# Two transposes of 256 x 1024 fp32, done by DMA in two-byte halves instead of by TensorE

## The chip, the cores and the metric

The kernel runs on one core of a Trainium2 chip. The metric is the device time of one execution in microseconds; three executions of the kernel before took 959.39 to 959.93 us, with a median of 959.49.

## What is computed

The program runs two transformer blocks, one after the other, on one sequence of 256 tokens and 1,024 channels in fp32. Two places matter for this change: the second block takes in a memory of 256 tokens for its cross-attention, and its last step adds a feed-forward to a residual that is the output. Cut to these:

```python
x = x + 0.5 * swiglu(rms_norm(x), ...)           # first block's second feed-forward ("f2u", "f2d")
h = rms_norm(x)                                  # and on to the second block
...
mn = rms_norm_2(mem, norm_mem)                   # mem: 256 tokens x 1024
xkv = mn @ xa_w_kv
...
h = h + (silu(g_conv) * (fn @ ffn_w_up)) @ ffn_w_down   # last feed-forward ("f3u", "f3d")
return h                                         # 256 tokens x 1024, one row a token
```

## The kernel before

Activations are kept transposed in SBUF: `xT` holds the residual as 8 groups of 128 channels (partitions) by 256 tokens, and every product streams such a tile. Weights come as slabs of 8 x 256 or, in the down projections, 11 x 256 columns; SyncE loads slab `s` into `raw[s % 2]`. For accuracy each fp32 product is made of three: ScalarE rounds a slab into a high part `wh` (`split_hi`), VectorE subtracts it for a low part `wl` (`split_lo`), each in two halves (1,536 and 1,280 columns in a down projection), and TensorE forms ah x wh, al x wh and ah x wl. `wh` and `wl` have two slots as well, so the split of slab `s + 2` follows TensorE's use of slab `s`, and TensorE waits for a half of `wl` before it takes that half up. The instructions of each engine are in the order in which the code writes them; there is no scheduler.

A down projection makes its output in four quarters `q` of 256 channels, each from two slabs, `s + 2 q` and `s + 2 q + 1`, of 66 matmuls each. Each engine goes through the quarters in its own `feed_forward`: in quarter 0 ScalarE and VectorE split slab `s + 2`, with which TensorE begins quarter 1. Hooks named `between` are called in each quarter.

**The memory** lies in `memraw` with tokens on partitions. In the down projection `f2d`, between the first and the second quarter, TensorE transposes it (`memory_in`, which calls `transpose_in`, 16 transposes of 128 x 128) into four PSUM banks; ScalarE (`memory_hi`) and VectorE (`memory_lo`) make the high and low parts `mo`, `mlo` from them in quarters 1 and 2. One quarter's matmuls also have a matmul of 32 columns in them (`narrow`) whose result is not used.

**The residual.** In the last down projection `f3d` the output is made with tokens on partitions, so that it can be stored in rows. The residual `xT` is transposed for it by TensorE (`rows_of_x`, 16 transposes) in the second product of `f3u`, just behind the last update of `xT`. ScalarE (`rows_in`) and VectorE (`rows_added`) copy it from PSUM to `xtok`. In `f3u` TensorE's product needs a free accumulator; it is freed by VectorE's line 2104, which waits for the norm's factor, a reciprocal (line 2063).

Of the kernel before, what the change touches and what calls it, by code (L numbers as in the profile page):

```python
# [18 lines left out]
P = 128  # L19
# [50 lines left out]
def shared_signals():  # L70
# [11 lines left out]
    for kind, signals, each, stages in kinds:  # L82
# [7 lines left out]
        "mixer2_dve": [("e7", 1), ("mem_lo", 4), ("kpe", 1), ("la_lo", 1), ("rho2", 1), ("kv_e", 1), ("kv_rd", 1), ("akv", 1),  # L90
# [6 lines left out]
        "mixer2_pe": [("mem_ps", 4), ("kv_ps", 1), ("uk_ps", 3), ("gl_z", 1), ("uq_ps", 3), ("kq_T", 8),  # L97
# [36 lines left out]
def build(nc, A, consts, out):  # L134
# [5 lines left out]
    with ctx:  # L140
# [91 lines left out]
        rin = sb("rin", [P, 2, 4])  # L232
        ah = sb("ah", [P, DC, T], f32r)
# [6 lines left out]
        with ExitStack() as sc:  # L240
# [26 lines left out]
            with ExitStack() as s2:  # L267
                ch = sb("ch", [P, DC, T], f32r, scope=s2)
                cl = sb("cl", [P, DC, T], f32r, scope=s2)

# [44 lines left out]

        L = [ctx.enter_context(nc.psum_tensor(f"acc{i}", [P, 512], f32)) for i in range(2)]
# [35 lines left out]
        xtok = ytok  # L352
        yl = xn[:, :, :].rearrange("p c t -> p (c t)").rearrange("p (g f) -> p g f", g=2)[:, :, 512:1024]\
# [295 lines left out]
        def _(pe):  # L649
# [82 lines left out]
            def rows_of_x():  # L732

                acc_freed(pe, ACC0["xo"] + 2)
                acc_freed(pe, ACC0["xo"] + 3)
                for b in range(TB):
                    for g in range(2):
                        for c in range(4):
                            ins = nc.tensor.transpose(Q[1 + 2 * b + g][:, c * P:(c + 1) * P],
                                                      xT[:, 4 * g + c, b * P:(b + 1) * P], ident)  # L740
                        ins.then_inc(S("res_ps"), 1)

            def late(st):

                if st == "n8":
                    return lambda k: k == 6 and (rows_of_x(), norm_spread(st))
                return lambda k: k == 6 and norm_spread(st)
# [54 lines left out]
            def opening(name, st, xh, xl, extra=None):  # L802
# [51 lines left out]
            def feed_forward(up, down, st, between=None, tokens=False):  # L854
# [13 lines left out]
                for q in range(4):  # L868
# [583 lines left out]
        def _(act):  # L1452
# [279 lines left out]
            def memory_hi(q):  # L1732

                if q == 0:
                    act.wait_ge(*signal("mem_in", 16))
                    for b in range(TB):
                        if b:
                            act.wait_ge(*signal("mem_sq", b))
                        A_(stmp[:, :, :].rearrange("p a t -> p (a t)"), memraw[:, b, :], ACT.Square, scale=1.0 / 32,
                           accum_out=ms7[:, b:b + 1]).then_inc(S("mem_sq"), 1)  # L1740
                elif q < 3:
                    for j in (2 * q - 2, 2 * q - 1):
                        act.wait_ge(*signal("mem_ps", j + 1))
                        for c in range(2):
                            ins = A_(mo[:, 2 * j + c, :], Q[2 + j][:, c * T:(c + 1) * T], ACT.Copy, scale=col(V_MEM + 2 * j + c))
                        ins.then_inc(S("mem_hi"), 1)
# [280 lines left out]
        def _(dve):  # L2027
# [64 lines left out]
            def feed_forward(up, down, st, conv=False, low=None, between=None):  # L2092
# [52 lines left out]
                looped(dve, FP, body, peel=2 if conv else 1)  # L2145
                s, n = SLAB0[down], ACC0[down]
# [21 lines left out]
            def rows_added(q):  # L2168
# [3 lines left out]
                if q == 0:  # L2172
                    for k in range(2):
                        dve.wait_ge(*signal("res_ps", 2 * k + 2))
                        V.tensor_copy(xtok[:, k, 512:D], Q[2 + 2 * k][:, :]).then_inc(S("rows_d"), 1)
                    dve.wait_ge(*signal("rows_a", 2))
                    dve.wait_ge(*signal("rows_d", 2))
# [330 lines left out]
            def memory_lo(q):  # L2508

                if q == 0:  # L2510
                    dve.wait_ge(*signal("mem_sq", 2))
                    V.tensor_scalar(e7[:, :], ms7[:, 0:2], EPS, EPS, ADD, MUL).then_inc(S("e7"), 1)
                elif q < 3:
                    for j in (2 * q - 2, 2 * q - 1):
                        dve.wait_ge(*signal("mem_hi", j + 1))
                        for c in range(2):
                            k = 2 * j + c
                            ins = V.scalar_tensor_tensor(mlo[:, k, :], Q[2 + j][:, c * T:(c + 1) * T], col(V_MEM + k), f(mo[:, k, :]), MUL, SUB)
# [514 lines left out]
```

## Time and profile before

| | before |
|---|---|
| median of three executions | 959.49 us |
| the profiled execution | 959.49 us |
| its span, first to last instruction | 957.7 us |
| granted TensorE clock | 1.00 of full speed |
| TensorE busy | 952.7 us, 99% |
| VectorE busy | 698.4 us, 73% |
| ScalarE busy | 537.6 us, 56% |
| GpSimd busy | 125.9 us, 13% |

The span is read off the instruction records of one execution; 1.8 us of the device time lie around it. Busy times of the engines overlap each other, so they don't add up to the span; the engine that is busy for nearly all of it is the one whose work and whose waits count.

### The profile page before, as it was taken

How to read it: one execution, taken by the hardware profiler on the slowest of the kernel's cores; microseconds unless marked ns; L12 is line 12 of the kernel's file. 1: busy time of each engine (PE TensorE's matmuls, PEld its weight loads, DVE VectorE, ACT ScalarE, POOL GpSimd, SP SyncE). 2: the span in 40 equal slices, each digit the busy share in tenths (PEclk: the TensorE clock that was granted, in tenths of full speed). 3: DMA queues.
4: the chain of work that ended last, by engine and by line, in shares of the span. 5: the costliest groups of instructions: out<-in, count | busy, mean ns of one | idle time of the engine just before them, and what ended most of it. 6: DMA issues, size and time to landing. Idle time of an engine off the chain costs nothing.

```text
span 957.7 us, 20451 instructions
## 1 busy us (share of the span) xinstructions
PE 952.7 (99%) x8266; PEld 938.1 (98%) x8266; DVE 698.4 (73%) x1090; ACT 537.6 (56%) x783; POOL 125.9 (13%) x87
## 2 busy tenths in 40 slices
PE   9999999999999999999999999999999999999998
PEld 8999999999999999999999999999999999999998
DVE  5677657477879968877776656688698898887752
ACT  7454454356558964455545465587576674545531
POOL 0111110010036100002111112310002021223100
PEclk9999999999999999999999999999999999999999
DMA  8865675555454454575666665355245355655761
GB/s 264 253 210 176 188 252 167 185 176 179 152 194 140 141 168 133 177 263 176 193 201 198 222 202 178 95 159 175 89 139 172 131 177 174 211 187 177 254 208 65
DMA packets 169167, 172.42 MB, mean 180 GB/s; under 512 B 5748, under 2 KB 167054, under 8 KB 168974
## 3 DMA queue, kind: packets, MB, share of 16 engines
q1 hardware_dynamic: 168270, 170.70, 55.4%
q8 instruction: 48, 0.79, 0.4%
q10 hardware_dynamic: 832, 0.79, 0.3%
q14 instruction: 17, 0.14, 0.1%
HBM read 170.42 MB, written 1.06 MB: 179 GB/s over the span
## 4 chain that ended last, share of the span: by engine, by line
PE 99%; DMA 1%; SPq 0%; DVE 0%; issue 0%; ACT 0%
PE acc L798 87%; PE part L848 1%; PE acc L848 1%; PE part L890 1%; PE part L914 1%; DMA xraw<-in_x 1%; PE part L1204 1%; PE part L900 1%; PE acc L671 1%; PE part L1194 0%; PE part L1227 0%; PE part L1013 0%; PE part L1406 0%; PE part L936 0%; PE part L1214 0%; PE part L1260 0%
## 5 line engine op out<-in xcount | busy, mean ns | idle before, releaser
L464 ACT ACTIVATE wh<-raw 128x1024 fp32r<-128x1024 f32 (+2 forms) x291 | 316.4, 1112 | 269.0 <-PE acc L798 119.2
L483 DVE TENSOR_TENSOR wl<-raw,wh 128x1024 fp32r<-128x1024 f32 (+2 forms) x292 | 393.1, 1385 | 47.2 <-ACT wh L464 46.6
L798 PE MATMUL acc<-ah,wh 128*128 128x256 f32 x1504 | 415.0, 279 | 0.0
L798 PE MATMUL acc<-al,wh 128*128 128x256 f32 x1504 | 409.1, 276 | 0.0
L798 PE MATMUL acc<-ah,wl 128*128 128x256 f32 x1496 | 406.2, 277 | 0.0
L798 PEld LDWEIGHTS acc<-ah,wh 128*128 128x128 f32 x1504 | 282.0, 188 | 3.3 <-issue 2.5
L798 PEld LDWEIGHTS acc<-al,wh 128*128 128x128 f32 x1504 | 280.4, 188 | 0.0
L798 PEld LDWEIGHTS acc<-ah,wl 128*128 128x128 f32 x1496 | 278.0, 188 | 0.1
L798 PE MATMUL acc<-hh,wh 128*128 128x256 f32 x352 | 97.3, 277 | 0.0
L798 PE MATMUL acc<-hh,wl 128*128 128x256 f32 x352 | 97.2, 276 | 0.0
L798 PE MATMUL acc<-hl,wh 128*128 128x256 f32 x352 | 97.2, 276 | 0.0
L2959 POOL TENSOR_TENSOR sil<-sil,rstd 128x512 f32<-128x512 f32 x32 | 56.3, 1760 | 304.0 <-ACT sil L1530 212.5
L2940 POOL TENSOR_TENSOR sq<-sq 128x512 f32<-128x512 f32 x15 | 27.5, 1833 | 316.3 <-ACT sq L1461 260.2
L798 PEld LDWEIGHTS acc<-hh,wh 128*128 128x128 f32 x352 | 66.1, 188 | 0.0
L798 PEld LDWEIGHTS acc<-hl,wh 128*128 128x128 f32 x352 | 66.1, 188 | 0.0
L798 PEld LDWEIGHTS acc<-hh,wl 128*128 128x128 f32 x352 | 66.1, 188 | 0.0
L2135 DVE TENSOR_TENSOR hid<-acc,sil 128x512 f32<-128x512 f32 x33 | 22.8, 691 | 42.4 <-PE acc L798 26.7
L2104 DVE TENSOR_TENSOR sil<-acc,rstd 128x512 f32<-128x512 f32 x22 | 15.2, 692 | 31.8 <-PE acc L798 31.7
L798 PE MATMUL acc<-wh,ah 128*128 128x256 f32 x128 | 36.7, 287 | 0.1
L798 PE MATMUL acc<-wh,hh 128*128 128x256 f32 x132 | 36.4, 276 | 0.0
L798 PE MATMUL acc<-wh,hl 128*128 128x256 f32 x132 | 36.4, 276 | 0.0
L798 PE MATMUL acc<-wl,hh 128*128 128x256 f32 x132 | 36.4, 276 | 0.0
(476 smaller groups left out, 1557.2 us busy)
## 6 DMA issues: line engine op xcount, KB each, us to landing
raw<-in_ffn_w_down SPq DMA_DIRECT2D x24, 1408.0 KB, 6.4
raw<-in_w_in SPq DMA_DIRECT2D x33, 1024.0 KB, 5.3
raw<-in_ffn_w_gate SPq DMA_DIRECT2D x32, 1024.0 KB, 5.3
raw<-in_ffn_w_up SPq DMA_DIRECT2D x32, 1024.0 KB, 5.4
raw<-in_w_out SPq DMA_DIRECT2D x8, 1024.0 KB, 5.2
raw<-in_w_proj_attn SPq DMA_DIRECT2D x4, 1024.0 KB, 5.2
raw<-in_w_proj_mlstm SPq DMA_DIRECT2D x4, 1024.0 KB, 5.5
raw<-in_xa_w_kv SPq DMA_DIRECT2D x4, 1024.0 KB, 5.2
```

Of the source, the lines that this page charges most:

```text
L464: nc.scalar.activation(wh[:, slot, a * nw:b * nw], raw[:, slot, a * nw:b * nw], ACT.Copy).then_inc(S("w_hi"), 1)
L483: nc.vector.tensor_tensor(wl[:, slot, a * nw:b * nw], raw[:, slot, a * nw:b * nw], f(wh[:, slot, a * nw:b * nw]), SUB).then_inc(S("w_lo"), 1)
L671: ins = mm(o[:, m * T:(m + 1) * T], *three[q], start=first and k + m + q == 0, stop=last and k == 7 and m == 1 and q == which[-1], skip_gr ...
L798: ins = mm(dst, a, b, start=st and q == 0, stop=en_ and q == sweep[-1], skip_group_check=True)
L848: ins = mm(banks[m][:, 0:T], a, b, start=r + k + q == 0, stop=r == 1 and k == 10 and q == 2, skip_group_check=True)
L890: ins = mm(Q[hh_ % 2][:, (hh_ // 2) * 256:(hh_ // 2) * 256 + w], q, k, start=True, stop=True, skip_group_check=True)
L900: ins = nc.tensor.transpose(Q[2 + b][:, hh_ * P:(hh_ + 1) * P], prob[:, u % 2, hh_, b * P:(b + 1) * P], ident)
L914: ins = mm(bank[lo:hi, o0:o0 + P * len(hs)], v, x, start=b == 0 and o0 == 0, stop=b == units[u] - 1, skip_group_check=True)
L2104: V.tensor_tensor(gdst, two_t(L[n % 2][:, :]), factor, MUL).then_inc(free_sem(n), 1)
L2135: V.tensor_tensor(hid[:, :], L[(n + 1) % 2][:, :], sil[:, :], MUL).then_inc(free_sem(n + 1), 1)
L2940: G.tensor_tensor(sq[:, 0, :], sq[:, 0, :], sq[:, j, :], ADD).then_inc(S(st + "_ps"), 1)
L2959: G.tensor_tensor(two_t(sil[:, :]), two_t(sil[:, :]), factor, MUL).then_inc(S(up + "_sr"), 1)
```

## The change

Each fp32 word is cut into its two 16-bit halves. VectorE copies the halves into two planes (`mem_planes`), DMAs on ScalarE's queue transpose each plane (`dma_start_transpose`, in `mem_turned`), and VectorE puts the halves together again: for the memory back into `memraw`, for the residual into `xtok`. The planes of the memory are made at the end of `f2u`, and four transposing DMAs of 128 x 1,024 are issued; the planes of the residual are made at the end of `f3u`, and two of 128 x 2,048 are issued. `rows_of_x`, `memory_in` and the use of the 32-column matmul in `f2d` are gone.

```diff
@@ TensorE
-            def rows_of_x():
-                acc_freed(pe, ACC0["xo"] + 2)
-                acc_freed(pe, ACC0["xo"] + 3)
-                for b in range(TB):
-                    for g in range(2):
-                        for c in range(4):
-                            ins = nc.tensor.transpose(Q[1 + 2 * b + g][:, c * P:(c + 1) * P],
-                                                      xT[:, 4 * g + c, b * P:(b + 1) * P], ident)
-                        ins.then_inc(S("res_ps"), 1)
...
-                        product(s + 1, 0, 8, n + 1, xh, xl, before=lambda k: k == 1 and rows_of_x(), low_last=True,
+                        product(s + 1, 0, 8, n + 1, xh, xl, low_last=True,
                                 ahead=lambda: norm_everywhere(st))
...
-                                narrow=(1, Q[0]) if (st, q, r) in (("n1", 0, 1), ("n3", 1, 0)) else None)
+                                narrow=(1, Q[0]) if (st, q, r) == ("n1", 0, 1) else None)
...
-            def memory_in(q, r):
-                if (q, r) == (0, 1):
-                    pe.wait_ge(*signal("mem_in", 16))
-                    transpose_in(memraw, "mem_ps", Q[2:6])
-            feed_forward("f2u", "f2d", "n3", between=memory_in)
+            feed_forward("f2u", "f2d", "n3")
@@ ScalarE, memory_hi
+                    act.wait_ge(*signal("mem_pl", 1))
+                    for h in range(2):
+                        for b in range(TB):
+                            act.dma_start_transpose(mem_turned[:, h, :, b * P:(b + 1) * P], mem_planes[:, h, b, :]).then_inc(S("mem_tr"), 16)
                 elif q < 3:
+                    act.wait_ge(*signal("mem_T", 1))
                     for j in (2 * q - 2, 2 * q - 1):
-                        act.wait_ge(*signal("mem_ps", j + 1))
...
@@ ScalarE, rows_in
-                    for k in range(2):
-                        act.wait_ge(*signal("res_ps", 2 * k + 1))
-                        A_(xtok[:, k, 0:512], Q[1 + 2 * k][:, :], ACT.Copy).then_inc(S("rows_a"), 1)
+                    act.wait_ge(*signal("x_pl", 1))
+                    for h in range(2):
+                        act.dma_start_transpose(x_turned[:, h, :, :].rearrange("p b (k c) -> p (b k) c", k=DC),
+                                                x_planes[:, h, :, :, :].rearrange("p b k t -> p (b k t)")).then_inc(S("x_tr"), 16)
@@ VectorE, feed_forward, behind the last step of the up projection
+                if st == "n3":
+                    between(-1)
+                if conv:
+                    for k in range(4):
+                        acc_freed(dve, ACC0["xo"] + k)
+                    for h in range(2):
+                        ins = V.tensor_copy(x_planes[:, h, :, :, :].rearrange("p b k t -> p k b t"), xT_halves[:, h, :, :, :])
+                    ins.then_inc(S("x_pl"), 1)
@@ VectorE, rows_added
+                    dve.wait_ge(S("x_tr"), 32)
+                    for h in range(2):
+                        ins = V.tensor_copy(xtok_halves[:, h, :, :], x_turned[:, h, :, :])
+                    ins.then_inc(S("x_rows"), 1)
+                    dve.wait_ge(*signal("x_rows", 1))
@@ VectorE, memory_lo
+                if q < 0:
+                    dve.wait_ge(*signal("mem_in", 16))
+                    for b in range(TB):
+                        ins = V.tensor_copy(mem_planes[:, :, b, :], mem_halves[:, b, :, :])
+                    ins.then_inc(S("mem_pl"), 1)
+                elif q == 0:
                     dve.wait_ge(*signal("mem_sq", 2))
+                    dve.wait_ge(S("mem_tr"), 64)
+                    for h in range(2):
+                        ins = V.tensor_copy(memT_halves[:, h, :, :], mem_turned[:, h, :, :])
+                    ins.then_inc(S("mem_T"), 1)
```

VectorE around the entry into `f2d`. In the rows, `wl` is a low half of a weight slab (1,536 and 1,280 columns), `hl` the last low part of the hidden layer, and `xT` the sum of quarter 0. Before:

```order
L2143 TENSOR_TENSOR hl<-hid,hh 128x512
L483 TENSOR_TENSOR wl<-raw,wh 128x1536
L483 TENSOR_TENSOR wl<-raw,wh 128x1280
L2159 SCALAR_TENSOR_TENSOR xT<-acc,xT 128x512
L2512 TENSOR_SCALAR e<-ms 128x2
```

And in the changed kernel:

```order
L2143 TENSOR_TENSOR hl<-hid,hh 128x512
L2521 COPY mem_planes<-memraw 128x2x1024 x2
L496 TENSOR_TENSOR wl<-raw,wh 128x1536
L496 TENSOR_TENSOR wl<-raw,wh 128x1280
L2167 SCALAR_TENSOR_TENSOR xT<-acc,xT 128x512
L2527 COPY memraw<-mem_turned 128x2048 x2
L2529 TENSOR_SCALAR e<-ms 128x2
```

Two copies have come between `hl` and the split of slab `s + 2`, and two between the sum of quarter 0 and what follows it.

ScalarE at the same place, with the squares of the memory (`stmp,ms`), the high parts of slabs (`wh`) and the last high part of the hidden layer (`hh`). The changed kernel has:

```order
L1531 ACTIVATE hh<-hid 128x512
L1734 ACTIVATE stmp,ms<-memraw 128x1024 x2
L1739 DMA_TRANSPOSE mem_turned<-mem_planes 128x8x128 x4
L477 ACTIVATE wh<-raw 128x1536
L477 ACTIVATE wh<-raw 128x1280
```

Before, the split of slab `s + 2` stood right behind the squares; now the four DMAs stand between them, and the first of them waits for VectorE's planes. In `f3d` the places are the same: VectorE's two plane copies stand behind `hl` and ahead of the split, ScalarE's two DMAs ahead of its split.

## Rows read from the trace of the kernel before

**Rows 1.** The page: the span, and busy us, share and instructions of each engine.

```profile
span 957.7 us, 20451 instructions
...
PE 952.7 (99%) x8266; PEld 938.1 (98%) x8266; DVE 698.4 (73%) x1090; ACT 537.6 (56%) x783; POOL 125.9 (13%) x87
```

**Rows 2.** The chain in order of time, 540 to 700: start, us, what.

```profile
568.23 1.75 PE part L936 x16
...
570.68 0.12 PE part L779
570.80 50.78 PE acc L798 x448
```

**Rows 3.** The same chain, 762 to 905.

```profile
778.64 1.75 PE part L739 x16
...
785.88 1.65 PE acc L798 x12
```

**Rows 4.** VectorE's timeline, 550 to 625: start, us, instructions, idle before.

```profile
557.97 0.69 DVE L2143 TENSOR_TENSOR hl<-hid,hh 128x512 fp32r<-128x512 f32 x1
561.12 3.16 DVE L483 TENSOR_TENSOR wl<-raw,wh 128x1536 fp32r<-128x1536 f32 x2 [2.47 <-ACT wh L464]
568.27 0.69 DVE L2159 SCALAR_TENSOR_TENSOR xT<-acc,xT 128x512 f32<-128x512 f32 x1 [3.98 <-PE acc L798]
...
575.83 1.76 DVE L483 TENSOR_TENSOR wl<-raw,wh 128x1536 fp32r<-128x1536 f32 x1 [3.73 <-ACT wh L464]
```

**Rows 5.** ScalarE's timeline in the same stretch.

```profile
558.57 0.18 ACT L1739 ACTIVATION_READ_ACCUMULATOR stmp<-memraw 128x1 f32 x1
...
564.92 1.50 ACT L464 ACTIVATE wh<-raw 128x1536 fp32r<-128x1536 f32 x1 [2.67 <-PE acc L798]
```

**Rows 6.** VectorE's timeline ahead of the last feed-forward.

```profile
776.53 6.90 DVE L483 TENSOR_TENSOR wl<-raw,wh 128x1024 fp32r<-128x1024 f32 x4 [0.67 <-ACT wh L464]
783.36 1.74 DVE L2063 RECIPROCAL rstd<-std 128x256 f32<-128x256 f32 x1
785.13 0.69 DVE L2104 TENSOR_TENSOR gpad<-acc,rstd 128x512 f32<-128x512 f32 x1
```

**Rows 7.** VectorE's groups by shape: busy us, mean ns; idle before.

```profile
L2868 DVE TENSOR_SCALAR prob<-prob,rin 128x256 f32<-128x256 f32 x8 | 2.3, 351 | 0.1
...
L2668 DVE TENSOR_SCALAR prob<-prob,rin 128x128 f32<-128x128 f32 x8 | 1.8, 282 | 0.1
...
L2753 DVE COPY xkt<-acc 128x512 f32<-128x512 f32 x2 | 1.4, 690 | 0.4 <-PE acc L798 0.4
...
L2555 DVE COPY rstd<-part 128x256 f32<-128x256 f32 x1 | 0.4, 425 | 1.0 <-PE part L728 1.0
```

**Rows 8.** VectorE's timeline at the last down projection.

```profile
900.86 0.68 DVE L2143 TENSOR_TENSOR hl<-hid,hh 128x512 fp32r<-128x512 f32 x1
```

**Rows 9.** TensorE's timeline where each second output quarter begins.

```profile
568.06 1.15 PE L936 MATMUL part<-cst,memraw 128*128 128x128 f32 x9
...
909.99 0.28 PE L798 MATMUL acc<-wh,hh 128*128 128x256 f32 x1
```

**Rows 10.** DMAs: issue durations (ACTq, SPq); KB each, us to landing.

```profile
L1578 ACTq DMA_DIRECT2D raw<-in_ffn_w_gate x3: 412/481/491, 1.4 to 2.4; - x3
...
raw<-in_w_in SPq DMA_DIRECT2D x33, 1024.0 KB, 5.3
...
780.65 0.37 SPq L591 DMA_DIRECT2D raw<-in_ffn_w_up  x1
```

**Rows 11.** TensorE's timeline over a short stop.

```profile
388.56 0.28 PE L798 MATMUL acc<-eh,wl 128*128 128x256 f32 x1
388.81 0.36 PE L798 MATMUL acc<-bh,wh 128*128 128x256 f32 x1
389.01 0.28 PE L798 MATMUL acc<-bl,wh 128*128 128x256 f32 x1
...
389.48 0.28 PE L798 MATMUL acc<-bh,wl 128*128 128x256 f32 x1
```

More of the change, by code:

```diff
@@ L89, in shared_signals @@
     chains = {
-        "mixer2_dve": [("e7", 1), ("mem_lo", 4), ("kpe", 1), ("la_lo", 1), ("rho2", 1), ("kv_e", 1), ("kv_rd", 1), ("akv", 1),
+        "mixer2_dve": [("mem_pl", 1), ("mem_T", 1), ("e7", 1), ("mem_lo", 4), ("kpe", 1), ("la_lo", 1), ("rho2", 1), ("kv_e", 1), ("kv_rd", 1), ("akv", 1),
                        ("rho7", 1), ("k_ss", 4), ("k_ms", 1), ("eq", 1), ("kt", 1), ("qt", 1), ("gl_cum", 2),
@@ L96, in shared_signals @@
                        ("sog", 1), ("gl_sq", 2), ("gl_sd", 1), ("xf_sd", 1)],
-        "mixer2_pe": [("mem_ps", 4), ("kv_ps", 1), ("uk_ps", 3), ("gl_z", 1), ("uq_ps", 3), ("kq_T", 8),
+        "mixer2_pe": [("kv_ps", 1), ("uk_ps", 3), ("gl_z", 1), ("uq_ps", 3), ("kq_T", 8),
                       ("gl_keT", 1), ("gl_att", 1), ("gl_dS", 3), ("gl_o", 2), ("go_T", 2), ("xq_ss", 2)],
@@ L232, in build @@
         rin = sb("rin", [P, 2, 4])
+        u16 = mybir.dt.uint16
         ah = sb("ah", [P, DC, T], f32r)
@@ L269, in build @@
                 cl = sb("cl", [P, DC, T], f32r, scope=s2)
+        with ExitStack() as sc:
+            mem_planes = sb("mem_planes", [P, 2, TB, D], u16, scope=sc)
+            mem_turned = sb("mem_turned", [P, 2, DC, T], u16, scope=sc)
         mo = sb("mo", [P, DC, T], f32r)
@@ L314, in build @@
                 xph = sb("xph", [P, TB, 4, T], f32r, scope=s1)
+        x_planes = mem_planes[:, :, :, :].rearrange("p h b (k t) -> p h b k t", k=DC)
+        x_turned = mem_turned[:, :, :, :].rearrange("p h k t -> p h (k t)").rearrange("p h (b c) -> p h b c", b=TB)
+        xT_halves = xT[:, :, :].bitcast(u16).rearrange("p k (b t h) -> p h k b t", b=TB, h=2)
+        mem_halves = memraw[:, :, :].bitcast(u16).rearrange("p b (c h) -> p b h c", h=2)
+        memT = memraw[:, :, :].rearrange("p b c -> p (b c)").rearrange("p (k t) -> p k t", k=DC)
+        memT_halves = memraw[:, :, :].bitcast(u16).rearrange("p b c -> p (b c)").rearrange("p (k t h) -> p h k t", k=DC, h=2)
         L = [ctx.enter_context(nc.psum_tensor(f"acc{i}", [P, 512], f32)) for i in range(2)]
@@ L352, in build @@
         xtok = ytok
+        xtok_halves = xn[:, :, :].bitcast(u16).rearrange("p c t -> p (c t)").rearrange("p (b f h) -> p h b f", b=TB, h=2)
         yl = xn[:, :, :].rearrange("p c t -> p (c t)").rearrange("p (g f) -> p g f", g=2)[:, :, 512:1024]\
@@ L730, in norm_spread @@
                 ins.then_inc(S(st + "_sp"), 1)
-            def rows_of_x():
-                acc_freed(pe, ACC0["xo"] + 2)
-                acc_freed(pe, ACC0["xo"] + 3)
-                for b in range(TB):
-                    for g in range(2):
-                        for c in range(4):
-                            ins = nc.tensor.transpose(Q[1 + 2 * b + g][:, c * P:(c + 1) * P],
-                                                      xT[:, 4 * g + c, b * P:(b + 1) * P], ident)
-                        ins.then_inc(S("res_ps"), 1)
             def late(st):
-                if st == "n8":
-                    return lambda k: k == 6 and (rows_of_x(), norm_spread(st))
                 return lambda k: k == 6 and norm_spread(st)
@@ L2172, in rows_added @@
                 if q == 0:
[L2173 to L2177, printed above, removed]
+                    dve.wait_ge(S("x_tr"), 32)
[3 more added lines that the diff above has]
+                    dve.wait_ge(*signal("x_rows", 1))
                 if q < 3:
@@ L2508, in memory_lo @@
             def memory_lo(q):
-                if q == 0:
+                if q < 0:
[4 more added lines that the diff above has]
+                elif q == 0:
                     dve.wait_ge(*signal("mem_sq", 2))
+                    dve.wait_ge(S("mem_tr"), 64)
+                    for h in range(2):
+                        ins = V.tensor_copy(memT_halves[:, h, :, :], mem_turned[:, h, :, :])
+                    ins.then_inc(S("mem_T"), 1)
                     V.tensor_scalar(e7[:, :], ms7[:, 0:2], EPS, EPS, ADD, MUL).then_inc(S("e7"), 1)
@@ L2517, in memory_lo @@
                             k = 2 * j + c
-                            ins = V.scalar_tensor_tensor(mlo[:, k, :], Q[2 + j][:, c * T:(c + 1) * T], col(V_MEM + k), f(mo[:, k, :]), MUL, SUB)
+                            ins = V.scalar_tensor_tensor(mlo[:, k, :], memT[:, k, :], col(V_MEM + k), f(mo[:, k, :]), MUL, SUB)
                         ins.then_inc(S("mem_lo"), 1)
```

2 lines of the change are left out of this document (1 added, 1 removed).

## The prediction

> **What bounds the kernel now.** I read the page's busy times first. TensorE is busy 952.7 of 957.7 us, VectorE 698.4, ScalarE 537.6 [rows 1]. So only TensorE's own instructions, or a wait of TensorE, can move the end. The second view is the chain that ended last, in order of time. In it the reader should see two blocks of 16 transposes lying in the middle of long runs of matmuls: the memory's at 568.23, 1.75 us long, and the residual's at 778.64, also 1.75 us [rows 2, 3]. That is 109 ns for one. The third view is the timeline of VectorE and ScalarE where the change puts its new work: in the first quarter of the second feed-forward's down projection [rows 4, 5], and in the same place of the last feed-forward [rows 8]. The question at each place is when VectorE has the low half of the third slab (`split_lo(s + 2)`) ready, because TensorE needs it when its second output quarter starts: at 568.06, where its transposes begin now, in the one, at 909.99 in the other [rows 9]. The profiled execution took 959.49 us with its 1.8 us around the span, which is also the median, so the sums are made against 959.49.
>
> **What is removed at the memory.** 16 transposes, 1.75 us, and the 32-column matmul behind them, 0.12 us [rows 2]: 1.87 us. TensorE's work follows from its own matmuls here, VectorE adding the accumulator as soon as it is done at 568.27 [rows 4], so this gain is whole if nothing new makes TensorE wait.
>
> **What is removed at the residual.** Also 1.75 us of transposes, but this gain I take at nothing. TensorE runs into the wait for its accumulator right after: it takes up the third product of the last feed-forward at 785.88 [rows 3], and the accumulator is freed by VectorE's L2104 at 785.13 + 0.69 = 785.82 [rows 6]. VectorE comes to it from the reciprocal (783.36, 1.74 us) and to that from four weight splits that start at 776.53 and run 6.90 us without a hole [rows 6]. None of these waits for the transposes. If TensorE is done 1.75 us earlier it waits 1.7 us longer; 0.06 us is the most that can be won.
>
> **What is added on VectorE.** At each place two copies of 2,048 two-byte elements per partition that make the planes, and two that put the transposed halves back; the removed PSUM copies of the residual (two of 690 ns) are the small change. The trace has no two-byte copy. From SBUF to SBUF one source goes at 351 ns for 256 columns and 282 for 128 [rows 7], 0.53 ns an element; from PSUM a copy takes 425 ns for 256 and 690 for 512, 1.04 ns an element. So 2,048 elements cost between 0.35 + 1792 x 0.53 = 1.30 us and 0.69 + 1536 x 1.04 = 2.28 us. I take 1.30, since these copies too stay in SBUF with one source. The Trainium skill (VectorE: DVE Perf Modes, the modes' conditions) says that a one-source operation within SBUF takes two elements a cycle, and four only if both sides are 16-bit with step one, which the strided halves are not; the two slopes in the rows agree with its first half, and the sum by it would be the same.
>
> **What is added on ScalarE.** ScalarE issues the transposing DMAs, four of 256 KB at the memory, two of 512 KB at the residual, ahead of `split_hi(s + 2)`. All that is queued behind them on ScalarE waits: that split, and behind it VectorE's split and TensorE. The trace has no such DMA. Below, a plain issue on ScalarE's queue took 481 ns [rows 10]. Above, the issue may hold ScalarE for as long as the bytes take: 1 MB lands in 5.3 us [rows 10], so 1.3 us for 256 KB and 2.65 us for 512 KB. I take the upper end, 5.2 and 5.3 us in all, since a transpose of 128 x 1024 has to be cut into many small blocks, for which a plain copy's 0.48 us is the wrong row. The Trainium skill (DMA: Bandwidth & Descriptors, the table of cycles before and after) gives 262,144 sequencer cycles for 8,192 tiles from SBUF to SBUF, 32 a tile, and 512 cycles for a plain copy. SyncE's plain issue of 0.37 us [rows 10] makes such a cycle 0.72 ns, and by that page, as an estimate, the 256 tiles of one place would hold ScalarE for 5.9 us; the sum by it would be 967.0.
>
> **The memory, step by step.** VectorE ends `hl` at 557.97 + 0.69 = 558.66 [rows 4]. Planes: + 2 x 1.30 = 561.26. ScalarE is free from 558.75 [rows 5], issues until 566.5, then splits: high half of the first part 1.50 us [rows 5], 568.0; VectorE's low half 1.76 us [rows 4], 569.76. TensorE stands ready at 568.06: a wait of 1.70 us. The old schedule had the same low half from 561.12 [rows 4], so it was far from late. The next slab: VectorE's second part ends at 571.2, the accumulator's add at 571.9, the two copies back at 574.5 (the DMAs, issued by 566.5, have landed by then if they need less than 5.4 us more), the next low half at 576.3; TensorE wants it at 569.76 + 66 x 0.118 = 577.5. No second wait.
>
> **The pace after a wait.** After even a short wait TensorE runs slower until a matmul of another width comes. In the rows it stops for 0.14 us at 388.56, and then starts a matmul each 117 ns ((389.48 - 389.01) / 4) where it did each 113 before [rows 11]; the run of 448 in which the 32-column matmul stands ahead has 50.78 / 448 = 113.3 ns [rows 2]. The change takes that 32-column matmul away at the memory. So with a wait there the 448 matmuls up to 621.6 cost 448 x 4.4 ns = 1.97 us. Memory in all: - 1.87 + 1.70 + 1.97 = + 1.80 us.
>
> **The residual, step by step.** VectorE ends `hl` at 900.86 + 0.68 = 901.54 [rows 8]; planes 904.1; ScalarE issues until 909.4; high 910.9; low 912.7. TensorE stands ready at 909.99 [rows 9]: 2.7 us. The copies back (to 916.9 behind the second part of the split), the add (0.69) and the next low half end at 919.3, TensorE wants it at 912.7 + 7.8 = 920.5. The 396 matmuls to the end at the slower pace: 1.74 us. In all + 4.44 us. It is more than at the memory, since from the end of `hl` to the moment that TensorE stands ready there are 8.45 us here (901.54 to 909.99) and 9.40 there (558.66 to 568.06), and since no gain stands against it.
>
> **Sum.** 959.49 + 1.80 + 0 + 4.44 = 965.7 us.
>
> **The rivals.**
> 1. *The issues are cheap* (0.48 us each). Then 561.26 + 1.9 + 1.50 + 1.76 = 566.4 is ahead of 568.06, and 904.1 + 1.0 + 3.25 = 908.3 ahead of 909.99. No wait, no slower pace, only the 1.87 us of the memory stay: 957.6 us, on the other side. It decides from the point at which the four issues take under 3.5 us together, and the two under 2.6. For it speaks that plain issues are done in under half a microsecond; and the Trainium skill (Advanced Engine Details and Errata, the section on the X-bar transpose) says transposing DMAs are as fast as ordinary ones, which tells of their bytes and not of the engine that issues. 22 in 100.
> 2. *Issues held and copies at the slow rate* (2.28 us). Memory: planes 563.2, issues 568.4, low half 571.7, a wait of 3.6; then the copies back end at 578.4 and the next low half at 580.3 against 579.5, 0.8 more. Residual: 4.6 and 0.8. With 3.7 of pace and - 1.87: 971.1 us. Against it stands the 0.53 ns slope of the rows. 15 in 100.
> 3. *The pace stays at 113 ns*, only the waits come: 965.7 - 3.7 = 962.0 us. 10 in 100.
> 4. *The transposed halves land late*, over 5 us after their issue, since the loads of the next slabs share the 16 queues. VectorE then stands in its wait with all splits behind it, and the time is beyond 971.5. 8 in 100.
> 5. *Cheap issues, slow copies.* Memory: low half at 568.4, 0.3 of wait, then the copies back make the next slab late by 1.2; about the same at the residual: - 1.87 + 1.5 + 1.2 and some pace, 960 to 963. 5 in 100.
>
> The forecast itself holds 40 in 100.
>
> **The numbers.** Rival 1 lies at the lower end and can't be left out, rival 2 at the upper: 957.4 to 971.5. The forecast's own range is 962.5 to 967.5. A measurement of this kernel tells about 0.2%, 1.9 us, from no change: 957.57 and 961.41. Rival 1 falls on the first of these bounds, so its 22 are shared: 13 faster, 9 same. Same gets 8 more from rivals 3 and 5 and from a forecast whose terms are half of what I take. Slower 70.
>
> **What would show it.** The DMA transposes on ScalarE's queue at 561 with 1.3 us between them, and no split of ScalarE from 561 to 566; VectorE's copies of 1.3 us; a wait of TensorE of 1.7 us at the start of the second quarter and 2.7 in the last stage; 117 to 118 ns a matmul behind each; and TensorE's third product of the last feed-forward no earlier against VectorE's L2104 than now. The prediction is wrong if ScalarE takes up its split within 2 us of the planes, if the copies take over 2 us, or if that third product starts 1.7 us earlier than the memory's gain explains.

## The result, and the profile after

The changed kernel takes 969.06 us (median; 967.55 to 970.32), the kernel before 959.51 us (959.39 to 959.93) beside it. The ratio is 1.0097, interval 1.0083 to 1.0111: slower by 1%, on the forecast side, by 9.6 us where 6.2 were forecast. The time lies inside the whole range (up to 971.5 us), but above the forecast's own part of it (up to 967.5).

The page of the changed kernel, as [rows 1]: TensorE has 33 instructions fewer and is busy 2.8 us more. The last line is ScalarE's DMA queue.

```profile
span 967.4 us, 20397 instructions
...
PE 955.5 (99%) x8233; PEld 940.6 (97%) x8233; DVE 702.0 (73%) x1096; ACT 536.4 (55%) x781; POOL 130.3 (13%) x87
...
q10 hardware_dynamic: 9216, 2.89, 1.5%
```

Fewer instructions and more busy time means that the instructions left have become slower. Where, the chain in order of time shows. Around the memory it reads as follows (start, us, what), where [rows 2] had nothing but TensorE:

```profile
558.22 0.60 DVE hl L2143
558.82 2.28 DVE mem_planes L2521 x2
...
561.12 1.33 ACTq L1739
...
562.48 2.06 ACTq L1739
...
564.58 1.34 ACTq L1739
...
565.95 2.23 ACTq L1739
...
568.27 1.49 ACT wh L477
...
569.79 1.77 DVE wl L496
...
571.69 53.35 PE acc L798 x454
```

The reader is to see that for over 13 us the end of the kernel hangs on no matmul. VectorE's `hl`, its two planes (1.14 us apart), four issues on ScalarE's queue, ScalarE's high half, VectorE's low half, and only then TensorE, which had been ready at 568.22: its last matmul ahead of the gap starts at 568.11 and the next at 571.69, so it waited 3.58 - 0.11 = 3.47 us. The four issues take 7.05 us, from 561.12 to 568.17. The last down projection shows the same chain, with two issues, 5.52 us in all:

```profile
904.99 2.29 DVE mem_planes L2152 x2
...
907.30 3.54 ACTq L2020
...
910.87 1.95 ACTq L2020
...
912.92 1.49 ACT wh L477
...
914.44 1.77 DVE wl L496
...
916.34 32.82 PE acc L798 x264
```

Here TensorE's starts lie 3.01 us apart, from 913.34 to 916.34, a wait of 2.9 us. The granted clock behind each wait, by windows (stretch, length, TensorE's busy us and instructions, granted clock, DMA share, GB/s):

```profile
572.70:576.10 3.40, 3.40 (x19) 0.51 0.55 160
577.00:617.00 40.00, 40.00 (x355) 1.00 0.55 175
917.40:920.80 3.40, 3.40 (x18) 0.51 0.58 161
929.00:949.00 20.00, 20.00 (x172) 1.00 0.56 179
```

In the first and the third line TensorE is busy all the time, at a granted clock of 0.51, the level of 1.2 GHz: most of the matmuls start 213 ns apart instead of 113. This begins 1.0 and 1.1 us after TensorE, having stood for 3.5 and 2.9 us, takes up work again. At each place 17 matmuls take 3.53 us in place of 17 x 0.1133, which costs 1.6 us. At the memory, where the matmuls between the wait and this fall are slower too (0.118 us each), it is 1.7 us in all. After it the clock is back at 1.00. The second line has 355 instructions in 40 us, as the kernel before has in the same window (356): the pace there is the fast one. The last has 172 in 20 us, against 179 before: there the slow pace has come.

Between the two places, where the residual's 16 transposes went, VectorE runs through the same rows as in [rows 6], each 3.47 us later:

```profile
780.01 6.89 DVE L496 TENSOR_TENSOR wl<-raw,wh 128x1024 fp32r<-128x1024 f32 x4 [0.66 <-ACT wh L477]
786.82 1.74 DVE L2063 RECIPROCAL rstd<-std 128x256 f32<-128x256 f32 x1
788.60 0.69 DVE L2104 TENSOR_TENSOR gpad<-acc,rstd 128x512 f32<-128x512 f32 x1
```

TensorE's timeline has two waits there now, 1.26 and 0.27 us, by the profile's own count, which [rows 3] did not have:

```profile
784.73 0.70 PE L734 MATMUL part<-sq,cst 128*128 128x256 f32 x2 [1.26 <-POOL sq L2971]
...
789.34 0.39 PE L798 MATMUL acc<-ah,wh 128*128 128x256 f32 x1 [0.27 <-DVE gpad L2104]
```

Together 1.53 us: that is where nearly all of the 1.75 us of the removed transposes went.

To compare the stages of all runs, one table is worked out from TensorE's records: the time from the first matmul of the second down projection to the first matmul on `kr` of the next stage, and from the first matmul of the last down projection to TensorE's last. A slow start or end elsewhere does not enter it. Each row is of one execution, which need not be the median one: for the issues behind ScalarE's split it is the fastest (968.92 us, the other three took 972.0 to 972.1), for the later copies the slowest (963.16, median 958.98), in which the memory's stage begins 4.3 us later than before.

| kernel | memory's stage, us | last stage, us |
|---|---|---|
| before | 69.12 | 59.73 |
| changed | 72.42 | 65.95 |
| memory alone | 72.93 | 59.73 |
| residual alone | 69.12 | 64.33 |
| both, issued behind ScalarE's split | 70.31 | 67.91 |
| plain DMAs in place of transposing ones | 67.23 | 59.73 |
| memory early | 67.23 | 59.73 |
| both early | 67.23 | 59.73 |
| memory behind, copies back later | 68.49 | 59.73 |
| plain, four squares more | 71.42 | 59.73 |
| plain, three and five squares more | 70.42 | 65.96 |
| sizes exchanged | 71.23 | 66.49 |
| memory on SyncE's queue | 67.23 | 59.73 |
| both on SyncE's queue | 67.23 | 62.51 |

Without a wait the memory's stage is 67.23: the removed work was worth 1.89 us, 1.87 by [rows 2]. From the end of the memory's stage to the start of the last one it is 272.7 to 273.1 us in thirteen of the fourteen kernels (residual alone 273.4), with the residual's transposes (before 272.80, memory on SyncE 272.79, memory early 273.12) and without them (changed 272.79, both early 273.09). So the losses of the changed kernel are 3.30 us in the one stage and 6.22 us in the other, 9.52 us in all, the whole of it. (The profiled execution took 970.32 us, but its span of 967.4 is that of the median execution, 967.3.)

### The profile page after: what moved, and what is told of

The parts are those of the page before. It is cut to its first block, busy times and chain, and to the rows that moved or that the text cites. A ratio compares the mean times of both kernels' runs of the same rounds, so it can differ in the third digit from the quotient of the medians.

```text
span 967.4 us, 20397 instructions
## 1 busy us (share of the span) xinstructions
PE 955.5 (99%) x8233; PEld 940.6 (97%) x8233; DVE 702.0 (73%) x1096; ACT 536.4 (55%) x781; POOL 130.3 (13%) x87
## 3 DMA queue, kind: packets, MB, share of 16 engines
HBM read 170.42 MB, written 1.06 MB: 177 GB/s over the span
## 4 chain that ended last, share of the span: by engine, by line
PE 82%; issue 12%; DVE 2%; ACTq 1%; ACT 1%; POOL 1%; DMA 0%; POOLq 0%; SPq 0%; DVEq 0%
PE acc L798 71%; DVE wl L496 1%; PE part L848 1%; PE acc L848 1%; ACTq L1739 1%; PE part L890 1%; PE part L914 1%; PE acc L684 1%; PE part L1199 1%; ACTq L2020 1%; ACT wh L477 1%; PE part L900 1%; DMA xraw<-in_x 0%; PE part L1189 0%; POOL sil L2976 0%
## 5 line engine op out<-in xcount | busy, mean ns | idle before, releaser
L496 DVE TENSOR_TENSOR wl<-raw,wh 128x1024 fp32r<-128x1024 f32 (+2 forms) x292 | 388.4, 1370 | 56.4 <-ACT wh L477 55.9
L2976 POOL TENSOR_TENSOR sil<-sil,rstd 128x512 f32<-128x512 f32 x32 | 59.2, 1851 | 301.3 <-ACT sil L1525 211.3
```

The source lines that it names most:

```text
L496: nc.vector.tensor_tensor(wl[:, slot, a * nw:b * nw], raw[:, slot, a * nw:b * nw], f(wh[:, slot, a * nw:b * nw]), SUB).then_inc(S("w_lo"), 1)
L2976: G.tensor_tensor(two_t(sil[:, :]), two_t(sil[:, :]), factor, MUL).then_inc(S(up + "_sr"), 1)
```

## The experiments

### One part alone

Two kernels: only the memory through DMA, the residual's transposes back where they stood, and the reverse. The diff of each is half of the change.

> Only the memory goes by DMA; the residual is transposed by TensorE as before. Theory (ScalarE is held by the issues of the transposing DMAs, 7 us here, TensorE waits 3.5 us for the split behind them and then runs at half clock for 3.4 us, which costs 1.8 us more): - 1.87 + 3.5 + 1.8, so 3.4 us slower than before, 962.9 us. Rival (the two places disturb each other, or the time is lost where the trace shows no wait): more than 5 us slower.

> Only the residual goes by DMA; the memory is transposed by TensorE as before. Theory: nothing is gained where the 16 transposes leave (TensorE waits for its accumulator instead), 2.9 us of wait, 1.8 us of half clock and 1.5 us of slower pace are lost in the last stage: 6.2 us slower, 965.7 us. Rival (the 1.75 us of the removed transposes are a real gain): 4.4 us slower, 963.9 us.

Memory alone: 964.14 us (963.08 to 965.41), ratio 1.0047 (1.0030 to 1.0064). Residual alone: 964.44 us (962.64 to 967.03), ratio 1.0048 (1.0032 to 1.0064), both against 959.9. The losses of the medians, 4.2 and 4.5 us, add up to 8.8 of the 9.6. The memory was forecast at 1.8 and costs 3.8 in its stage: TensorE waits 4.0 us, as the issues took 7.58 us here, and has the half clock behind it; the expectation of this run, 962.9 us, was 1.2 us too low. The residual, forecast at 4.4 and expected at 6.2 in this run, costs 4.6: a wait of 2.8 us, no stretch at half clock, and the slow pace to the end, 1.8 us. This is the forecast's sum within 0.2 us; what it lacked at the residual in the changed kernel (6.2) is the half clock.

### No transposing

```diff
-act.dma_start_transpose(mem_turned[:, h, :, b * P:(b + 1) * P], mem_planes[:, h, b, :])
+act.dma_start(mem_turned[:, h, 4 * b:4 * b + 4, :].rearrange("p k t -> p (k t)"), mem_planes[:, h, b, :])
```

The residual's two likewise. The same bytes are copied and nothing is transposed, so the output is made from untransposed halves.

> As the changed kernel, but the six DMAs copy the planes without transposing them (the output is made from untransposed halves; same bytes, same place in ScalarE's queue). Theory (it is the transposing form of the issue that holds ScalarE, not the bytes): each issue takes 0.5 us, no wait of TensorE, 957.6 us. Rival (ScalarE is held for as long as the bytes move): issues of over 1 us and a time above 962 us.

957.78 us (957.52 to 958.71), ratio 0.9977 (0.9968 to 0.9987). ScalarE's timeline (ACTq is its queue):

```profile
560.80 2.54 ACTq L1739 DMA_DIRECT2D mem_turned<-mem_planes  x4
563.45 4.04 ACT L477 ACTIVATE wh<-raw 128x1536 fp32r<-128x1536 f32 x3 [4.84 <-issue]
```

Four plain issues of the same 256 KB take 2.54 us, four transposing ones 7.05. ScalarE splits at 563.45 instead of 568.27 and TensorE waits nowhere. So planes, copies back and the landing of plain DMAs cost nothing where they stand; the loss starts from what a transposing DMA adds to its issue.

### The issues behind ScalarE's split

```diff
                     split_hi(act, s + 2 * q + 2)
+                    if st == "n3" and q == 0:
+                        act.wait_ge(*signal("mem_pl", 1))
+                        for h in range(2):
+                            for b in range(TB):
+                                act.dma_start_transpose(mem_turned[:, h, :, b * P:(b + 1) * P], mem_planes[:, h, b, :])
```

The residual's two stand there likewise, for "n8".

> Both places by DMA, but ScalarE issues the transposes behind its split of slab s + 2 in place of ahead of it; all else is as in the changed kernel. Theory (the order on ScalarE's queue is the whole loss): no wait of TensorE at either second quarter, the memory's 1.87 us are gained, the residual gives nothing: 957.6 us. Rival (VectorE's four copies, or the share of the DMA queues that the transposes take, make the splits late anyway): above 961 us.

972.0 us (968.92 to 972.1), ratio 1.0127 (1.0110 to 1.0143): no faster than the change itself, and slower by the median. The theory that the order on ScalarE's queue is the whole loss fell. The chain at the memory:

```profile
565.58 8.35 DMA mem_turned<-mem_planes
...
574.01 2.53 DVE memraw L2530 x2
...
576.59 1.67 DVE wl L496
...
578.30 44.26 PE acc L798 x388
```

The last issue and its landing take 8.35 us, VectorE then copies 2.53 us, and only behind that stands its low half of the fourth slab, for which TensorE has waited since 575.3: 2.96 us. VectorE's queue has taken the place of ScalarE's. At the residual the halves land 9.66 us after the second issue's start, and TensorE waits 4.4 us. In the changed kernel the later splits had kept the next slab's load back until 573.12; here it left at 564.17. The two transposes issued ahead of it landed 4.6 and 4.1 us after their issue, the two behind it 8.9 and 8.4 us. That the load is the reason was not tested apart.

Behind the memory's wait of 3.0 us neither the half clock nor the slow pace came: 320 matmuls go in the 36 us from 579 to 615, and the stage is 3.1 us above 67.23, the wait alone.

### Early, and later

In the first kernel the memory's planes are copied in the second and third pass of the up projection and one DMA is issued in each of the four passes behind; the second does the same for the residual too. The third keeps the issues behind ScalarE's split and moves the copies back, and their readers, one quarter later.

```diff
+if st == "n3" and isinstance(i, int) and 3 <= i < 7:
+    act.wait_ge(*signal("mem_pl", 2))
+    h, b = divmod(i - 3, 2)
+    act.dma_start_transpose(mem_turned[:, h, :, b * P:(b + 1) * P], mem_planes[:, h, b, :])
...
-                elif q == 0:
+                elif q == 1:
                     dve.wait_ge(*signal("mem_sq", 2))
...
-                elif q < 3:
-                    for j in (2 * q - 2, 2 * q - 1):
+                elif q > 1:
+                    for j in (2 * q - 4, 2 * q - 3):
```

> The residual as in the kernel before; the memory's planes are copied in the second and third pass of the second feed-forward's up projection, and its four transposing DMAs are issued one in each of the four passes behind them, some 60 to 100 us ahead of their first reader. Theory (the whole loss at the memory is the chain of planes, issues and split between the end of hl and the second quarter): no wait of TensorE at 568, the full 1.87 us of the removed work stay, 957.6 us. Its issues then stand alone and show whether 1.3 us (the estimate) or 1.76 us (the mean of the changed kernel) is the price without neighbours. Rival (transposing DMAs cost more than their bytes and hold back the weight loads wherever they stand): TensorE waits for slabs in the up projection, 960 us or more.

> As the last one, and the residual too by DMA, planes in the third and fourth pass of the last up projection, the two issues in the fifth and sixth. Theory (the residual's transposes stood where TensorE would wait anyway): nothing more than the memory's gain, 957.6 us, with a wait of 1.5 us ahead of the third product of the last feed-forward. Rival A (the 1.75 us are won): 955.9 us. Rival B (VectorE is busy 82 parts in 100 there and 1.2 us more in a pass make TensorE wait): over 959.5 us.

> The residual as before; the memory's DMAs behind the split of the third slab on ScalarE (as in the run with both behind), and the copies back behind VectorE's share of the fifth slab, one quarter later, with their readers a quarter later too. In the run with both behind TensorE waited 3.08 us at the third quarter, since VectorE stood from 568.7 to 574.0 for the landing and then copied 2.5 us ahead of its split. Theory (that blocked queue of VectorE was the whole loss): no wait, 957.6 us. Rival (ScalarE's 8.5 us of issues are themselves too late for the next slab's high half): a wait of 1 us or more at the third quarter, 959 to 961 us.

Memory early: 957.93 us (957.34 to 959.8), ratio 0.9981 (0.9972 to 0.9990). Both early: 957.69 us (957.22 to 958.41), ratio 0.9977 (0.9968 to 0.9986), the same within the interval: the residual's transposes are worth nothing, as the forecast had it. The issues by ScalarE's timeline, the memory's and then the residual's (of the kernel with both early):

```profile
471.40 1.33 ACTq L1530 DMA_TRANSPOSE mem_turned<-mem_planes  x1
...
504.04 1.07 ACT L477 ACTIVATE wh<-raw 128x1024 fp32r<-128x1024 f32 x1 [1.40 <-PE acc L811]
```

```profile
823.49 3.71 ACTq L1521 DMA_TRANSPOSE mem_turned<-mem_planes  x1
...
834.55 3.96 ACTq L1521 DMA_TRANSPOSE mem_turned<-mem_planes  x1
```

A 256 KB transpose that stands alone takes 1.25 to 1.33 us to issue, the forecast's 1.3. Four in a row took 1.33, 2.06, 1.34 and 2.23: every second one is dearer. A 512 KB one takes 3.3 to 4.0 us alone or first in the row, and as the second 1.95 in the changed kernel and 5.2 where the issues stood behind the split. The price does not follow the bytes alone.

Copies later: 958.98 us (958.69 to 963.16), ratio 0.9992 (0.9983 to 1.0001). No wait in either half of the second quarter, as the theory had it, but its price was wrong: TensorE waits 1.06 us at 621.2, the start of the next stage, since the memory's readers on VectorE (`mlo`) now stand in front of what that stage needs (`al`).

### A wait without transposing DMAs

To part the wait from its source, ScalarE was made late by squares of 1.1 us ahead of plain DMAs: four at the memory in one kernel, three there and five at the residual in another. The output is made from untransposed halves, as above.

```diff
+                    for j in range(4):
+                        if j:
+                            act.wait_ge(S("more_sq"), j)
+                        A_(stmp[:, :, :].rearrange("p a t -> p (a t)"), memraw[:, j % 2, :], ACT.Square,
+                           scale=1.0 / 32).then_inc(S("more_sq"), 1)
```

> The kernel with plain DMAs in place of the transposing ones (its output is made from halves that were not transposed), and at the memory four more squares on ScalarE ahead of the issues, 1.2 us each, so that only ScalarE is late: the low half of the third slab at 571.5, a wait of TensorE of 3.4 us at 568.1. Theory (a wait of this length by itself brings the stretch at half clock behind it): 957.8 + 3.4 + 1.8 = 963.0 us. Rival A (the half clock came from the transposing DMAs): 961.2 us. Rival B (the slower pace of 117 to 118 ns up to the next narrow matmul, as the forecast had it): 963.2 us with no half clock.

> The kernel with plain DMAs (its output is made from halves that were not transposed), with three more squares on ScalarE at the memory and five at the residual, ahead of the issues. By the run with four, TensorE waits 1.4 us at the memory and 2.9 us at the residual. Theory: at the memory no half clock behind so short a wait, and 113 ns a matmul; behind the residual's wait the slower pace of 117.8 ns to the end, with or without transposing DMAs: 957.8 + 1.4 + 2.9 + 1.7 = 963.8 us. Rival (the slower pace at the residual came of the transposing DMAs): 962.1 us. If the short wait at the memory brings the half clock as well, 1.8 us more.

Four squares: 962.3 us (961.75 to 966.58), ratio 1.0034 (1.0020 to 1.0047). The squares delayed less than expected, TensorE waits 2.5 us. TensorE by windows, behind the wait:

```profile
573.00:576.00 3.00, 3.00 (x22) 0.74 0.97 319
577.00:617.00 40.00, 40.00 (x356) 1.00 0.53 168
```

The half clock comes behind the wait with no transposing DMA in the kernel, and after it stands the fast pace (356 in 40 us). Three and five squares: 967.46 us (965.26 to 968.36), ratio 1.0078 (1.0059 to 1.0097), over the 963.8 of the theory. At the memory, behind a wait of 1.1 us:

```profile
573.00:576.00 3.00, 3.00 (x28) 1.00 0.96 336
577.00:617.00 40.00, 40.00 (x342) 1.00 0.54 165
```

No half clock, but 342 matmuls in 40 us, which start 117.8 ns apart, up to the end of the stage: 70.42 - 67.23 - 1.1 = 2.1 us for a wait of 1.1. This is the forecast's "pace after a wait", and it is real. At the residual a wait of 2.9 us, the half clock (granted clock 0.50 from 914.3 to 917.2), and the slow pace: 6.23 us, the changed kernel's 6.22. So that stage is explained by TensorE's wait alone, whatever caused it.

Over all kernels, the half clock stood behind waits of 2.5, 2.9 (twice), 3.4, 3.5, 4.0 and 4.4 us, and not behind those of 1.1 (twice), 1.2, 1.9, 2.8 and 3.0. Nor did it stand behind the waits of 1.3 us ahead of the last up projection's third product, in nine kernels. Between 2.5 and 3.0 it goes both ways: the length of the wait alone does not decide it.

### Sizes exchanged

```diff
-                    for h in range(2):
-                        for b in range(TB):
-                            act.dma_start_transpose(mem_turned[:, h, :, b * P:(b + 1) * P], mem_planes[:, h, b, :])
+                    for h in range(2):
+                        act.dma_start_transpose(x_turned[:, h, :, :].rearrange("p b (k c) -> p (b k) c", k=DC),
+                                                mem_planes[:, h, :, :].rearrange("p b c -> p (b c)"))
```

The residual's reverse, in four. The copies back read the other layout.

> The changed kernel with the sizes of its transposing DMAs exchanged: the memory in two of 512 KB, the residual in four of 256 KB, all issued where they were. In the changed kernel four small ones held ScalarE 1.33, 2.06, 1.34 and 2.23 us (7.05 with the steps between), two large ones 3.54 and 1.95 us (5.52). Theory (the price is of the DMA's size and of its place in the row): the memory's two hold ScalarE 5.5 us and TensorE waits 2.0 us there instead of 3.5; the residual's four hold it 7.05 us and TensorE waits 4.4 us instead of 2.9. Rival (the price is of the place in the program, by what loads run beside it): 7.05 us at the memory and 5.5 us at the residual as before, the waits 3.5 and 2.9 us.

969.09 us (966.79 to 972.06), ratio 1.0101 (1.0075 to 1.0127): the same sum, otherwise distributed. ScalarE at the memory, and at the residual:

```profile
561.26 5.48 ACTq L1738 DMA_TRANSPOSE mem_turned<-mem_planes  x2
566.85 5.19 ACT L477 ACTIVATE wh<-raw 128x1536 fp32r<-128x1536 f32 x4 [7.79 <-issue]
```

```profile
906.19 6.04 ACTq L2021 DMA_TRANSPOSE mem_turned<-mem_planes  x4
```

Two large ones take 5.48 us at the memory, as the theory said, and the wait is 1.9 us; four small ones 6.04 us at the residual (1.27, 1.97, 1.34, 1.37), less than the 7.05 expected, and the wait is 3.4. Behind the memory's wait of 1.9 us there is no half clock but the slow pace (342 in 40 us). So the price goes mostly with size and place in the row; the fourth issue's 1.37 here against 2.04 to 3.66 elsewhere is open.

### On SyncE's queue

The last two kernels leave the issues where they were in time and change the queue: SyncE issues them behind the load of the fourth slab, first the memory's alone, then both.

```diff
                         load(s0 + k, 0, d[:, 11 * (k % 2):11 * (k % 2) + 11, k // 2 * 256:(k // 2 + 1) * 256])
+                        if k == 3:
+                            sp.wait_ge(*signal("mem_pl", 1))
+                            for h in range(2):
+                                for b in range(TB):
+                                    sp.dma_start_transpose(mem_turned[:, h, :, b * P:(b + 1) * P], mem_planes[:, h, b, :])
```

> The residual as in the kernel before; the memory's four transposing DMAs on SyncE's queue, behind the load of the fourth slab of the down projection and ahead of the fifth, where SyncE stands idle in its wait anyway. Theory (whoever issues is held as long, and what is queued behind is late): the issues take SyncE from 561 to 568, the third slab is split in time and TensorE doesn't wait at 568; the fifth slab's load starts at 568.2 instead of 564.2, lands 6.4 us later, and is split at 577.8 against 575.2 wanted: a wait of 2.6 us at the third quarter, 960.2 us. Rival (SyncE has the time to spare, or isn't held): no wait, 957.6 us.

Memory on SyncE's queue: 957.63 us (957.38 to 958.81), ratio 0.9980 (0.9970 to 0.9989). SyncE's queue and VectorE:

```profile
561.00 7.16 SPq L614 DMA_TRANSPOSE mem_turned<-mem_planes  x4
568.20 21.60 SPq L528 DMA_DIRECT2D raw<-in_ffn_w_down  x4
```

```profile
560.88 3.15 DVE L496 TENSOR_TENSOR wl<-raw,wh 128x1536 fp32r<-128x1536 f32 x2
...
570.56 2.61 DVE L2538 COPY memraw<-mem_turned 128x2048 uint16<-128x2048 uint16 x2 [1.55 <-DMA mem_turned<-mem_planes]
```

SyncE is held 7.16 us, as ScalarE was. VectorE's split stands at 560.88, as in [rows 4]. The rival was right and the expected wait wrong: the fifth slab, whose load leaves at 568.2, is wanted only at the third quarter's start, 583.3. (This expectation, and that of the kernel with later copies, call the second half of the second quarter the third quarter.)

> The changed kernel with nothing altered but the queue: the transposing DMAs of both places are issued by SyncE, behind the load of the fourth slab of each down projection. In the run with the memory's alone on SyncE it was held 7.16 us and TensorE didn't wait, since the load behind them is of the fifth slab, which is wanted only when the third quarter starts, 15 us after the second (the expectation of that run took it for the fourth slab, wanted 7.5 us after the second quarter's start, and was wrong in that). Theory: ScalarE's split is in time at the residual too, no wait of TensorE at either place: 957.7 us, and 59.7 us from the start of the last down projection to TensorE's last instruction, as before. Rival (the residual's rows land later than the accumulator's add at the first quarter's end, with VectorE's splits behind it): VectorE in its wait until 912 or later, then copies of 2.6 us, the fourth slab's low half at 917 against 915.8 wanted, a wait of about 1 us: 959 us.

959.59 us (957.28 to 961.78), ratio 0.9995 (0.9985 to 1.0005): the rival. VectorE at the residual:

```profile
912.24 2.60 DVE L2190 COPY xn<-mem_turned 128x2048 uint16<-128x2048 uint16 x2 [6.76 <-DMA mem_turned<-mem_planes]
914.87 0.69 DVE L2195 TENSOR_TENSOR xn<-acc,xn 128x512 f32<-128x512 f32 x1
915.48 6.22 DVE L496 TENSOR_TENSOR wl<-raw,wh 128x1536 fp32r<-128x1536 f32 x4
```

It stands 6.76 us for the landing, then come 2.6 us of copies and the add, and the low half is over 1 us late: a wait of 1.2 us and 1.6 us of slow pace behind it, 2.78 us together, more than the gain at the memory. This is one of the slower executions (960.84 us). Three took 957.3 to 957.4 us, the time without any wait; that the halves landed earlier in them is likely, but none of them has a trace.

## Why the prediction was right, and where its sizes were off

**The gain at the memory** (1.87 us) was right: 69.12 - 67.23 = 1.89 us in each kernel without a wait.

**The gain at the residual** (nothing) was right: TensorE waits where its transposes stood, and the stretch between is as long with as without them. But only 0.27 us of the wait is the one for the accumulator that the prediction named. The other 1.26 us come first and are a wait for GpSimd's sum of squares (`sq`), which it did not look at.

**VectorE's copies** (1.30 us each) were right: by the groups of the changed kernel 1.22 us each for the planes, 1.36 for the copies back at the memory and 1.33 at the residual. VectorE's timeline has the copies back at the memory and the next slab's low half behind them:

```profile
573.47 2.57 DVE L2527 COPY memraw<-mem_turned 128x2048 uint16<-128x2048 uint16 x2
...
575.96 3.19 DVE L496 TENSOR_TENSOR wl<-raw,wh 128x1536 fp32r<-128x1536 f32 x2
```

TensorE takes up that slab 66 matmuls and a stretch of half clock after 571.69, at about 581, and does not wait, as forecast ("no second wait").

**ScalarE's issues held** was right as a mechanism, and the memory's size the term that failed: 5.2 us forecast, 7.05 measured, so the wait came out 3.47 instead of 1.70. The price of one was right (1.25 to 1.33 us alone), and to take four times that was the error. The Trainium skill (DMA: Bandwidth & Descriptors, the table of cycles) led to an estimate of 5.9 us; four that stand alone took 5.1 us and four in a row 7.05, on either side of it. At the residual 5.3 us were forecast and 5.52 measured, the wait 2.7 and 2.9. The two issues did not share it as forecast: 3.54 and 1.95 us, not 2.65 each.

**The pace after a wait** was right in most places where it could be seen apart: 2.1 us at the memory behind a wait of 1.1 or of 1.9 us (forecast 1.97), 1.8 at the residual alone, behind 2.8 us (forecast 1.74). It is no general price: behind the 3.0 us at the memory, with the issues behind the split, the pace stayed fast. In the changed kernel another price stood behind the memory's wait, 1.7 us, nearly all of it half clock, and after it the fast pace. The two are about as dear, so the term came out near by luck.

**Missing** was the half clock. At the residual it came on top of the slow pace, 1.6 us.

By stages: memory - 1.89 + 3.47 + 1.72 = + 3.30 us (forecast + 1.80), residual 2.9 + 1.6 + 1.7 = + 6.2 us (forecast + 4.44). So the direction and the chain were right by the working. That 969.06 us fall inside the range is partly luck: the forecast's own part ends at 967.5, and it was rival 2, whose slow copies did not come, that stretched the range to 971.5.

**The rivals.** Rival 1 needed cheap issues, and is what the plain DMAs gave: 957.78 us for its 957.6. Rival 2's slow copies did not come. Rival 3 (the pace stays) holds behind none of the waits of one to two us in the down projections, and does hold behind the 3.0 us named above. Rival 4, halves that land late, was weighed for the order as changed and did not come there, since ScalarE was later still; it is what struck when the issues went behind the split or to SyncE.

Open: what makes every second 256 KB issue and the first 512 KB one dearer; why the clock fell behind a wait of 2.5 us and not behind one of 3.0; why the slow pace followed the half clock at the residual and not at the memory, and why neither came behind the 3.0 us in the kernel with the issues behind the split.

## What to carry to other kernels

Before moving work from a busy engine to a DMA, price the issue on the queue that issues it and name what stands behind it there; then follow the whole chain, landing and the copies that wait for it too, on every queue that it blocks, for with the order changed alone the loss only moved from ScalarE to VectorE. Put such a transfer where its inputs have long been ready (both early: 957.69 us, some 2 us faster than the kernel before and 11 us faster than the changed one) or on a queue that idles. A short stop of TensorE can cost far more than its length: 1.1 us of wait cost 3.2 here and 2.9 us cost 6.2, though 3.0 us at one place cost 3.1.

## What was not expected of the hardware

A transposing DMA's issue held its queue (ScalarE's and SyncE's alike) for 1.25 to 3.7 us for 256 KB and 1.95 to 5.2 us for 512 KB, by its place in the row, against 0.48 to 0.66 us for plain ones of the same size. Its landing was not slow in most kernels: 3.9 us after the issue (median) in the kernel with the memory early, 4.5 in the changed one, and 6.4 to 6.8 in the two with the issues behind the split. The Trainium skill (Advanced Engine Details and Errata, the section on the X-bar transpose) calls transposing DMAs as fast as ordinary ones. Plain ones in the same places landed after 4.4 us (256 KB) and 5.4 us (512 KB), against 4.1 to 4.7 and 4.4 to 5.5 for the transposing ones of the changed kernel, so these traces agree for the landing; where plain ones of 256 KB left 2 to 3 us later, behind the added squares, they landed after 2.7 and 3.0 us (medians). For the issue the traces do not agree.

Behind seven of the thirteen waits above TensorE's granted clock fell to half, at once or up to 1.1 us after it had taken up work again, and stayed there for 3.3 to 5.0 us though TensorE was busy throughout, with DMAs that transposed and with such that did not.
